# An encoder layer on one core: the square sum of r's first half goes from TensorE to GpSimd, and VectorE's work around the second up stage is reordered

## The chip, the cores and the metric

One core of one Trainium2 chip. The metric is the device time of one execution in microseconds. The kernel before has a median of 1065.91 us over three runs (1065.86 to 1066.0).

## The reference

One layer of a streaming encoder on 544 tokens (512 of a prompt and 32 of a sample), width 1024, all in float32:

```
r = x + 0.5 * rms_norm(swiglu_ffn(rms_norm(x, g1), w_up1, w_down1), g1_post)
z = rms_norm(r, g_mix) @ w_in                 # windowed attention and a gated short convolution
r = r + rms_norm(concat(norm_A(attn), norm_B(conv)) @ w_out, g_mix_post)          # stage "out"
r = r + 0.5 * rms_norm(swiglu_ffn(rms_norm(r, g2), w_up2, w_down2), g2_post)      # stages "up2", "down2"
r = r + rms_norm(sigmoid(rms_norm(r, g_ple) @ w_gate) * (p @ w_proj), g_ple_post)
```

`swiglu_ffn(x)` is `(silu(x @ gate) * (x @ up)) @ down` with a hidden width of 2816. Between the stages "out" and "up2" three things are needed of each token: the norm of out's result y, the sum r = r + norm(y), and the norm of the new r. The change lies there.

## The kernel before

**Tiling.** Features lie on the 128 partitions and tokens in the free dimension: r is eight tiles k = 0 to 7 of 128 features, each with two halves of 272 tokens, A and B. A float32 product is made of three matmuls in a reduced float32 type: each operand is split into a high part and the rest (w_hi x_hi, w_hi x_lo, w_lo x_hi). ScalarE makes the high parts (`split_hi` for weights, `high` for x), VectorE the rests (`split_lo`, `chain_lo`, whose results are x_lo). The normalising factor of x is not in x: the products are scaled by it afterwards on VectorE (`up_scale` makes tG and tU from the four PSUM banks, and by that frees the bank), so a matmul of up2 needs r alone, and its scaling needs the norm.

**Square sums.** ScalarE squares a tile of 272 tokens into one of two buffers `sq` (`square`, L684). GpSimd adds it to `ssq` (`add`, L602; the first of a sum is a copy, L599) and counts in the semaphore `summed`. ScalarE's square number s waits for `summed >= s - 1`, since the buffer must be free. When a sum is complete, TensorE multiplies `ssq` by a matrix of ones (`all_sums`, L1753), which adds over the partitions; ScalarE takes the root (`root`, L692), VectorE the reciprocal (`invert`, L1159). Sum 10 is y of half A, 11 is y of half B, 12 is r of half A, 13 is r of half B. **Sum 12 is the exception**: GpSimd is passed by. TensorE itself adds the eight squares in PSUM, one matmul by ones for each (`add_square`, L1760), with hooks in its passes over x_hi.

**Order around the change.** Every engine has a queue written out by hand.
- TensorE: the four products of out's half B (their ends are 3 us apart), then up2. For half A: a pass over x_hi of units 0 and 1, with sum 11 ahead of its fifth tile, a pass of units 2 and 3, both with the `add_square` hooks (all L1774), then the pass over x_lo for each of the four units (L1782). For half B (units 4 to 7): x_hi of all, then sum 13, then x_lo. After that products of 24 matmuls in turn (L1731, L1732, L1733), pair by pair: pairs 4 to 9, each of two products. A pair's product waits for the scaling (`g_scaled`, `u_scaled`) of the pair two before it. Behind pair 9 stand the seven products a round of a Strassen-like scheme (`seven`) for the rest of the hidden width, whose token operands (`scaled_x` and `token_block` on VectorE, L1212 and L1226) must be ready by then.
- ScalarE: evacuates out's products (square and copy of y), with r's high parts A between; then `root` 11, eight squares of r's half A, `root` 12, then high part and square of each tile of half B (`chain`), silu of pairs 0 and 1, and so on.
- VectorE: `chain_r` of half A (scale y by the norm, L1167, then r = y * gain + r, L1174), two `split_lo`, then reciprocal 11, `chain_r` of half B; after its tile 3 come the eight x_lo of half A, reciprocal 12 and `up_scale` of pair 0, after its tile 4 `up_scale` of pair 1. Then `scaled_x` of the block B21 (four instructions), the eight x_lo of half B, reciprocal 13, `split_lo`, `up_scale` of pairs 2 and 3, three more `split_lo` and token work, and `up_scale` of pair 4.

`up_stage` serves both up stages; `ci` is 0 in the first and 2 in the second.

Of the kernel before, what the change touches and what calls it, by code (L numbers as in the profile page):

```python
# [17 lines left out]
def encoder_layer(nc, t):  # L18
# [121 lines left out]


    SUM_HALF = [A, B] + [A, B, A, B] + [A, A, B, B] + [A, B, A, B] + [A, A, B, B] + [A, B]
    SUMMED = [8, 16, 30, 40, 38, 48, 52, 62, 60, 64, 76, 80, 88, 96, 110, 118, 120, 128, 140, 144]

    PLE_UNITS = [(i, h) for g in (0, 2) for h in (A, B) for i in (g, g + 1)]

# [6 lines left out]
    with ctx:  # L153
# [196 lines left out]

        TASKS_A = NCH + (HT - 1) // CHUNK + 1

        OUT_SQUARES = [(kind, h, k) for kind, n in (("y", KD // 2), ("r", KD)) for h in (A, B) for k in range(n)]

        MIX_SQUARES = [(0, k) for k in range(KA)] + [(n, k) for n in (1, 3) for k in (0, 1)] + \
                      [(2, k) for k in range(KA)] + [(n, k) for n in (1, 3) for k in (2, 3)]
# [100 lines left out]
        def sum_place(n):  # L457

            return 2 * (n % 2) if SUM0["mix"] <= n < SUM0["out"] else SUM_HALF[n]


        OWN_SUM = SUM0["out"] + 2

        def sums_asked(n):

            return n + 1 - (n > OWN_SUM)

        def sum_bank(n):

# [112 lines left out]
        def _(pool):  # L582
# [65 lines left out]
            for h in (A, B):  # L648
                run(SQ0["out"] + 4 * h, h, 4, True)
            for j, (kind, h, k) in enumerate(OUT_SQUARES):  # L650
                if (kind, h) == ("r", A):
                    continue
                add(SQ0["out"] + 8 + j, ssq[:, h, :], kind == "r" and k == 0)
            weight_sums(1, "up2")
            last_group(groups(SQ0["down2"], 2, DOWN_GROUPS), 2)
# [6 lines left out]
        def _(act):  # L662
# [22 lines left out]

            def root(n, size):

                if n == OWN_SUM:
                    act.wait_ge(summed, SUMMED[n])
                else:  # L690
                    act.wait_ge(sum_done, sums_asked(n))
                nc.scalar.activation(sum_bank(n), sum_bank(n), ACT.Sqrt, bias=eps[:], scale=1.0 / size)\  # L692
                    .then_inc(rooted, 1)

# [366 lines left out]
            def highs(first, last):  # L1061
                for k in range(first, last):
                    act.wait_ge(r_ready, 16 + k + 1)
                    high(2, k, A)

            out_evacuate(1, A, 0), out_evacuate(1, A, 1)
            split_hi(c1)
            out_evacuate(1, A, 2)
# [3 lines left out]
            split_hi(c1 + 2)  # L1072
            out_evacuate(1, B, 0)
            highs(0, 1)
            out_evacuate(1, B, 1)
            highs(1, 4)
            out_evacuate(1, B, 2)
            split_hi(c1 + 3)
            highs(4, KD)
            out_evacuate(1, B, 3)  # L1080
            root(SUM0["out"] + 1, D)
            for k in range(KD):
                square(half(r, k, A), squares + OUT_SQUARES.index(("r", A, k))).then_inc(squared, 1)
            root(SUM0["out"] + 2, D)

            act.wait_ge(state_stored, 16 * 6)
# [25 lines left out]

            def token_roots(k):

                act.wait_ge(sum_done, sums_asked(SUM0["ple"] + k))
                tiles, columns = TOKEN_SUMS[k]
                whole = [tt for tt in tiles if tt < XT - 1]
                i = nc.scalar.activation(rms_tok[:, whole[0]:whole[-1] + 1], columns[:, 0:len(whole)], ACT.Sqrt,
                                         bias=eps[:], scale=1.0 / D)
                if XT - 1 in tiles:  # L1120
                    i = nc.scalar.activation(rms_tok[0:DEC, XT - 1:XT], columns[0:DEC, len(whole):len(whole) + 1],
                                             ACT.Sqrt, bias=eps[0:DEC], scale=1.0 / D)
                i.then_inc(tok_rooted, 1)
# [25 lines left out]
        def _(dve):  # L1149
# [193 lines left out]
            def up_stage(n, s, d, ci, y, n_pre):  # L1343

                c0 = C0[s]
                if ci:
                    chain_r(ci, B, y, n_pre - 2, {3: lambda: (chain_lo(ci, A), invert(n_pre - 1, rpre[:, A, :]),
                                                              up_scale(s, 0)), 4: lambda: up_scale(s, 1)})
                    scaled_x(n, ci, B21)
                    chain_lo(ci, B)  # L1350
                    up_hidden(s, 0)
                else:
                    up_scale(s, 0)
                    chain_lo(ci, B, range(0, 2))
                    up_scale(s, 1)
                    up_hidden(s, 0), up_hidden(s, 1)
                    chain_lo(ci, B, range(2, KD))
                    scaled_x(n, ci, B21)
                invert(n_pre, rpre[:, B, :])
                if ci:  # L1360
                    up_hidden(s, 1)
                    split_lo(c0 + 4)
                    up_scale(s, 2)
                else:
                    up_scale(s, 2)
                    split_lo(c0 + 4)
                up_scale(s, 3)
                split_lo(c0 + 5)
                up_hidden(s, 2), up_hidden(s, 3)
                split_lo(c0 + 6), split_lo(c0 + 7)  # L1370
                if not ci:
                    rest_of_gains()
                scaled_x(n, ci, B11, B12)
                token_block(n, 0)
                scaled_x(n, ci, B22)
                up_pair(s, 4)
                token_block(n, 1), token_block(n, 2)
                token_block(n, 3)
                up_pair(s, 5)
                token_lo(n, 0), token_lo(n, 1)  # L1380
                up_pair(s, 6)
                split_lo(c0 + 8), split_lo(c0 + 9)
                first_sums(n, s, 0)
                token_lo(n, 2)
                up_pair(s, 7)
                block_lo(n, s, 0, 0)
                block_lo(n, s, 0, 1)
                block_lo(n, s, 0, 2)
                up_scale(s, 8)
                up_hidden(s, 8)  # L1390
                up_scale(s, 9)
                token_lo(n, 3)
                up_hidden(s, 9)
                token_lo(n, 4)
                block_lo(n, s, 0, 3)
                jobs(n, s, d)
# [256 lines left out]
            split_lo(EARLY[0]), split_lo(EARLY[1])  # L1653
            chain_r(2, A, y_out, SUM0["out"])
            split_lo(EARLY[2]), split_lo(EARLY[2] + 1)

            up_stage(1, "up2", "down2", 2, y_out, SUM0["out"] + 3)
            down_stage("down2", 3)
# [63 lines left out]
        def _(pe):  # L1722
# [15 lines left out]
            def all_sums(n, size=None):  # L1738
# [12 lines left out]
                    pe.wait_ge(attn_ready, NTASK)  # L1751
                src = ssm[:, k, :] if 0 <= k < 4 else ssq[:, SUM_HALF[n], :]
                nc.tensor.matmul(sum_bank(n), ones[:], src, start=True, stop=True).then_inc(sum_done, 1)  # L1753

            def add_square(n, k):

                s = SUMMED[n] - KD + k
                pe.wait_ge(squared, s + 1 - KD)
                pe.wait_ge(summed, s)
                nc.tensor.matmul(sum_bank(n), ones[:], sq[:, s % 2, :], start=(k == 0), stop=(k == KD - 1))\  # L1760
                    .then_inc(summed, 1)

            def hi_pass(pair, high, h, wait, hooks={}, ks=range(KD)):

# [93 lines left out]
            def up_stage(n, s, ci, hooks_hi, second, n_pre, after_b=lambda: None):  # L1858
                for h in (A, B):
                    units = [(U0[s] + 2 * p + m, C0[s] + 2 * PAIRS[p][0] + m, lambda p=p, m=m: up_ready(s, p, m))  # L1860
                             for p in (2 * h, 2 * h + 1) for m in range(2)]
                    if h == A and ci:
                        def high(k, h):
                            return x_high(ci, k, h)

                        def adds(first, last, at):
                            return {at + k - first: lambda k=k: add_square(OWN_SUM, k) for k in range(first, last)}
                        hi_pass(units[0:2], high, A, lambda k: pe.wait_ge(*hi_mark(ci, A, k)),
                                {4: lambda: all_sums(n_pre - 2), **adds(0, 2, 6)})
                        hi_pass(units[2:4], high, A, lambda k: None, adds(2, KD, 0))  # L1870
                        for m, (u, c, _) in enumerate(units):
                            lo_pass(u, c, lambda k, h: x_low(ci, k, h), A,
                                    None if m else lambda k: pe.wait_ge(x_ready, 16 * ci + k + 1))
                    elif h == A:

                        for m in range(4):
                            if m == 2:
                                turn_x(XT - 2), turn_x_sample()
                            hi_pass(units[m:m + 1], lambda k, h: x_high(0, k, h), A,
                                    lambda k: None if m else pe.wait_ge(*hi_mark(0, A, k)))  # L1880
                        first_sums()
                        for m, (u, c, _) in enumerate(units):
                            lo_pass(u, c, lambda k, h: x_low(0, k, h), A,
                                    None if m else lambda k: pe.wait_ge(x_ready, k + 1))
                    else:
                        if ci:
                            first_units(units, ci, B, lead=LEAD, between=lambda: all_sums(n_pre))
                        else:
                            first_units(units, ci, B, {}, {0: after_b}, between=lambda: all_sums(n_pre))
                for p in range(4, 2 * NCL):  # L1890
# [345 lines left out]
```

## Time and profile before

| what | value |
|---|---|
| median of three runs | 1065.91 us |
| the profiled execution | 1065.69 us |
| its span in the trace | 1063.9 us |
| outside the span | 1.8 us |
| TensorE, granted clock over the span | 0.994 |
| TensorE busy | 1035.0 us, 97% |
| VectorE busy | 701.3 us, 66% |
| ScalarE busy | 511.1 us, 48% |
| GpSimd busy | 278.5 us, 26% |

Times in the trace are from the start of the span. In a timeline each row is a start, a duration, the engine, line, operation and tiles, then in square brackets how long the engine had been idle and what ended that. Rows of several instructions ("x4") run from the start of the first to the end of the last. Ends overlap the next start by some 0.08 us on VectorE and ScalarE, and by more on TensorE, whose matmuls are pipelined; so spacing of starts is what an instruction costs its queue. The second up stage begins at 592.8 us.

### The profile page before, as it was taken

The numbers are of one execution on the slowest core, as the hardware profiler recorded it, in microseconds if no ns is written. First come the engines' busy times: TensorE is split into PE (matmuls) and PEld (weight loads), VectorE is DVE, ScalarE is ACT, GpSimd is POOL, SyncE is SP. The second block draws the span as 40 slices with busy tenths as digits, with TensorE's granted clock in tenths as the row PEclk, the third lists the DMA queues.
The fourth block names the chain that finished last, engine by engine and source line by source line (L and its number), as shares of the span: only waits on it lengthen the run. The fifth ranks groups of instructions, "written<-read, shape, count | busy, mean of one in ns | idle before, by whom it ended". The sixth has DMA issues, their size and how long they took to land.

```text
span 1063.9 us, 20130 instructions
## 1 busy us (share of the span) xinstructions
PE 1035.0 (97%) x8109; PEld 1012.7 (95%) x8109; DVE 701.3 (66%) x1053; ACT 511.1 (48%) x931; POOL 278.5 (26%) x214
## 2 busy tenths in 40 slices
PE   6999999999999999999999999999999999999896
PEld 6999999999999998888899999999999999999896
DVE  5889877777511269677695998977777841118743
ACT  5554555556412254434455555555555632126653
POOL 3114343431111142000323201443434021114311
PEclk9999999999999999999999999999999999999998
DMA  8214343335323303221234121443333632233002
GB/s 247 81 41 115 93 111 92 108 94 146 105 63 109 79 23 84 79 67 34 70 97 120 40 80 47 113 120 91 109 93 94 166 108 63 74 99 97 25 1 85
DMA packets 182679, 94.77 MB, mean 89 GB/s; under 512 B 11768, under 2 KB 180928, under 8 KB 182592
## 3 DMA queue, kind: packets, MB, share of 16 engines
q1 hardware_dynamic: 182576, 93.56, 31.8%
q8 instruction: 61, 1.00, 0.4%
q14 instruction: 26, 0.21, 0.1%
q10 hardware_dynamic: 16, 0.00, 0.0%
HBM read 91.15 MB, written 2.50 MB: 88 GB/s over the span
## 4 chain that ended last, share of the span: by engine, by line
PE 84%; DVE 9%; issue 2%; ACT 2%; POOL 1%; DMA 1%; SPq 1%; DVEq 0%; POOLq 0%; ACTq 0%
PE bank L1731 14%; PE bank L1733 14%; PE bank L1732 14%; PE bank L1852 9%; PE bank L1855 9%; PE bank L1854 9%; PE bank L1774 5%; PE bank L1782 2%; PE misc L1933 2%; PE misc L1852 1%; PE misc L1855 1%; PE misc L1854 1%; DVE x_lo L1183 1%; PE misc L2008 1%; DVE w_split L1153 1%
## 5 line engine op out<-in xcount | busy, mean ns | idle before, releaser
L1733 PE MATMUL bank<-h_hi,w_split 128*128 128x272 f32 x704 | 204.0, 290 | 0.0
L1731 PE MATMUL bank<-h_hi,w_split 128*128 128x272 f32 x704 | 203.0, 288 | 0.0
L1732 PE MATMUL bank<-h_lo,w_split 128*128 128x272 f32 x704 | 202.2, 287 | 0.0
L1153 DVE TENSOR_TENSOR w_split<-raw,w_split 128x1408 fp32r<-128x1408 f32 (+2 forms) x66 | 98.7, 1507 | 146.0 <-ACT w_split L679 146.0
L602 POOL TENSOR_TENSOR ssq<-ssq,sq 128x272 f32<-128x272 f32 x105 | 101.9, 970 | 234.9 <-ACT sq L684 228.9
L1732 PEld LDWEIGHTS bank<-h_lo,w_split 128*128 128x128 f32 x704 | 132.6, 188 | 0.1
L1731 PEld LDWEIGHTS bank<-h_hi,w_split 128*128 128x128 f32 x704 | 132.4, 188 | 0.1
L1733 PEld LDWEIGHTS bank<-h_hi,w_split 128*128 128x128 f32 x704 | 132.3, 188 | 0.0
L1852 PE MATMUL bank<-t_hi,even_blocks 128*128 128x272 f32 x432 | 125.3, 290 | 0.2
L1855 PE MATMUL bank<-t_hi,even_blocks 128*128 128x272 f32 x432 | 125.0, 289 | 0.0
L1854 PE MATMUL bank<-t_lo,even_blocks 128*128 128x272 f32 x432 | 124.4, 288 | 0.0
L632 POOL TENSOR_TENSOR s_rest<-s,raw_up 128x512 f32<-128x512 f32 x32 | 70.6, 2206 | 199.6 <-DVE s L1245 199.6
L679 ACT ACTIVATE w_split<-raw 128x1408 fp32r<-128x1408 f32 (+2 forms) x66 | 81.1, 1240 | 83.2 <-PE bank L1733 76.7
L1852 PE MATMUL bank<-t_hi,odd_blocks 128*128 128x272 f32 x384 | 111.5, 290 | 2.0 <-ACT kept L749 1.1
L1855 PE MATMUL bank<-t_hi,odd_blocks 128*128 128x272 f32 x384 | 111.1, 289 | 0.0
L1854 PE MATMUL bank<-t_lo,odd_blocks 128*128 128x272 f32 x384 | 110.5, 288 | 0.0
L1732 PE MATMUL bank<-x_lo,w_split 128*128 128x272 f32 x320 | 92.2, 288 | 0.0
L1852 PEld LDWEIGHTS bank<-t_hi,even_blocks 128*128 128x128 f32 x432 | 81.3, 188 | 0.6 <-issue 0.6
L1854 PEld LDWEIGHTS bank<-t_lo,even_blocks 128*128 128x128 f32 x432 | 81.4, 188 | 0.0
L1855 PEld LDWEIGHTS bank<-t_hi,even_blocks 128*128 128x128 f32 x432 | 81.3, 188 | 0.0
L1852 PEld LDWEIGHTS bank<-t_hi,odd_blocks 128*128 128x128 f32 x384 | 72.2, 188 | 2.7 <-issue 1.5
L1731 PE MATMUL bank<-x_hi_a,w_split 128*128 128x272 f32 x240 | 71.9, 299 | 1.5 <-DVE tG L1667 1.4
(253 smaller groups left out, 2626.3 us busy)
## 6 DMA issues: line engine op xcount, KB each, us to landing
raw_up<-w_ffn_gate_up SPq DMA_DIRECT2D x88, 512.0 KB, 5.1
raw<-w_ffn_down SPq DMA_DIRECT2D x32, 704.0 KB, 4.9
raw<-w_in SPq DMA_DIRECT2D x14, 512.0 KB, 4.2
raw<-w_ple_gate SPq DMA_DIRECT2D x8, 512.0 KB, 3.8
x_tok<-x_prompt SPq DMA_DIRECT2D x4, 512.0 KB, 5.1
raw<-w_in SPq DMA_DIRECT2D x8, 256.0 KB, 3.8
raw<-w_out SPq DMA_DIRECT2D x16, 128.0 KB, 3.5
raw<-w_out SPq DMA_DIRECT2D x8, 256.0 KB, 4.1
```

What stands on the lines that cost most here:

```text
L602: nc.gpsimd.tensor_tensor(dst, dst, sq[:, s % 2, :], ALU.add).then_inc(summed, 1)
L632: nc.gpsimd.tensor_tensor(s24(j)[:, 0, :], s31[:, 1, :], a[:, 0, :], ALU.add).then_inc(s24_made[n], 1)
L679: nc.scalar.activation(chunk_part(c, 0), chunk_raw(c), ACT.Copy).then_inc(hi_made, 1)
L1153: nc.vector.tensor_tensor(chunk_part(c, 1), chunk_raw(c), chunk_part(c, 0).bitcast(F32), ALU.subtract).then_inc(lo_made, 1)
L1731: nc.tensor.matmul(psum(u), wh, hi, start=(k == 0), stop=False)
L1732: nc.tensor.matmul(psum(u), wh, lo, start=False, stop=False)
L1733: mm = nc.tensor.matmul(psum(u), wl, hi, start=False, stop=(k == n - 1))
L1774: nc.tensor.matmul(psum(u), chunk_part(c, part)[:, k, :], high(k, h), start=(k == 0 and part == 0), stop=False)
L1782: mm = nc.tensor.matmul(psum(u), chunk_part(c, 0)[:, k, :], low(k, h), start=False, stop=(k == KD - 1))
L1852: nc.tensor.matmul(out, hi[:, k, :], x_h, start=(k == 0 and p in (1, 2, 7)), stop=False, skip_group_check=True)
L1854: nc.tensor.matmul(out, hi[:, k, :], x_l, start=False, stop=False, skip_group_check=True)
L1855: mm = nc.tensor.matmul(out, lo[:, k, :], x_h, start=False, stop=(k == 3), skip_group_check=True)
```

## The change

- TensorE: the eight `add_square` are gone. In their place one `all_sums` (sum 12) stands ahead of tile 5 of the second pass over x_hi of half A. Sum 13 stands behind the first x_lo pass of half B in place of ahead of it.
- GpSimd adds the eight squares of r's half A, as it does in all other sums. The order in which squares are added is: y of half B tile 0, r A 0, y B 1, r A 1 to 3, y B 2, y B 3, r A 4 to 7, r B 0 to 7. Sum 11 is therefore complete at `summed` 84 (80 before).
- ScalarE: the eight squares of r's half A are spread: tile 0 behind the first high part, tiles 1 to 3 behind high parts 1 to 3 and ahead of the evacuation of out's unit B 2, tiles 4 and 5 ahead of `root` 11, and 6 and 7 behind it.
- VectorE: four of the x_lo of half A come ahead of reciprocal 11, four remain behind tile 3 of `chain_r`. `scaled_x` of B21 moves from ahead of the x_lo of half B to behind `up_scale` 3 and its `split_lo`. The `split_lo` of chunk 4 comes ahead of reciprocal 13, and no longer behind it.

```diff
-    SUMMED = [8, 16, 30, 40, 38, 48, 52, 62, 60, 64, 76, 80, 88, ...]
+    SUMMED = [8, 16, 30, 40, 38, 48, 52, 62, 60, 64, 76, 84, 88, ...]
-        OUT_SQUARES = [(kind, h, k) for kind, n in (("y", KD // 2), ("r", KD)) for h in (A, B) for k in range(n)]
+        OUT_SQUARES = [("y", A, k) for k in range(KD // 2)] + \
+                      [("y", B, 0), ("r", A, 0), ("y", B, 1)] + [("r", A, k) for k in range(1, 4)] + \
+                      [("y", B, 2), ("y", B, 3)] + [(kind, h, k) for kind, h, a in (("r", A, 4), ("r", B, 0))
+                                                    for k in range(a, KD)]
 # GpSimd
             for j, (kind, h, k) in enumerate(OUT_SQUARES):
-                if (kind, h) == ("r", A):
-                    continue
                 add(SQ0["out"] + 8 + j, ssq[:, h, :], kind == "r" and k == 0)
 # ScalarE
             highs(0, 1)
+            squares_of_r(0, 1)
             out_evacuate(1, B, 1)
             highs(1, 4)
+            squares_of_r(1, 4)
             out_evacuate(1, B, 2)
             split_hi(c1 + 3)
             highs(4, KD)
             out_evacuate(1, B, 3)
+            squares_of_r(4, 6)
             root(SUM0["out"] + 1, D)
-            for k in range(KD):
-                square(half(r, k, A), squares + OUT_SQUARES.index(("r", A, k))).then_inc(squared, 1)
+            squares_of_r(6, KD)
             root(SUM0["out"] + 2, D)
 # VectorE
             split_lo(EARLY[2]), split_lo(EARLY[2] + 1)
+            chain_lo(2, A, range(0, 4))
...
                 if ci:
-                    chain_r(ci, B, y, n_pre - 2, {3: lambda: (chain_lo(ci, A), invert(n_pre - 1, rpre[:, A, :]),
-                                                              up_scale(s, 0)), 4: lambda: up_scale(s, 1)})
-                    scaled_x(n, ci, B21)
+                    chain_r(ci, B, y, n_pre - 2, {3: lambda: (chain_lo(ci, A, range(4, KD)),
+                                                              invert(n_pre - 1, rpre[:, A, :]), up_scale(s, 0)),
+                                                  4: lambda: up_scale(s, 1)})
                     chain_lo(ci, B)
                     up_hidden(s, 0)
+                    split_lo(c0 + 4)
...
                 if ci:
                     up_hidden(s, 1)
-                    split_lo(c0 + 4)
                     up_scale(s, 2)
...
                 up_scale(s, 3)
                 split_lo(c0 + 5)
+                if ci:
+                    scaled_x(n, ci, B21)
 # TensorE
-                                {4: lambda: all_sums(n_pre - 2), **adds(0, 2, 6)})
-                        hi_pass(units[2:4], high, A, lambda k: None, adds(2, KD, 0))
+                                {4: lambda: all_sums(n_pre - 2)})
+                        hi_pass(units[2:4], high, A, lambda k: None, {5: lambda: all_sums(n_pre - 1)})
-                            first_units(units, ci, B, lead=LEAD, between=lambda: all_sums(n_pre))
+                            first_units(units, ci, B, {}, {0: lambda: all_sums(n_pre)}, lead=LEAD)
```

## Rows read from the trace of the kernel before

**Rows 1.** The page's busy times: engine, us (share of the span), instructions.
```profile
PE 1035.0 (97%) x8109; PEld 1012.7 (95%) x8109; DVE 701.3 (66%) x1053; ACT 511.1 (48%) x931; POOL 278.5 (26%) x214
```
**Rows 2.** The chain that ended last, 592 to 620: start, us, what.
```profile
592.82 2.02 PE bank L1774 x16
...
596.32 0.63 PE misc L1760 x2
...
603.22 0.46 PE misc L1760 x2
...
609.14 8.00 PE bank L1774 x64
```
**Rows 3.** Timeline of TensorE, the first product of pair 4.
```profile
622.60 0.37 PE L1731 MATMUL bank<-x_hi_up,w_up 128*128 128x272 f32 x1 [0.75 <-DVE tG L1193]
```
**Rows 4.** Timeline of ScalarE, 587 to 596.
```profile
587.42 1.53 ACT L697 ACTIVATE x_hi_up<-r,gT 128x272 fp32r<-128x272 f32 x3
...
589.85 0.40 ACT L684 ACTIVATE sq<-bank 128x272 f32<-128x272 f32 x1 [0.90 <-PE bank L1733]
...
590.42 1.06 ACT L679 ACTIVATE w_up<-raw_up 128x1024 fp32r<-128x1024 f32 x1
591.37 1.75 ACT L697 ACTIVATE x_hi_up<-r,gT 128x272 fp32r<-128x272 f32 x4
593.03 0.38 ACT L684 ACTIVATE sq<-bank 128x272 f32<-128x272 f32 x1
...
595.35 0.46 ACT L692 ACTIVATE misc<-misc,eps 128x272 f32<-128x272 f32 x1 [1.65 <-PE misc L1753]
```
**Rows 5.** Timeline of GpSimd, 587 to 606.
```profile
587.33 0.77 POOL L602 TENSOR_TENSOR ssq<-ssq,sq 128x272 f32<-128x272 f32 x1 [2.23 <-ACT sq L684]
...
593.49 1.03 POOL L602 TENSOR_TENSOR ssq<-ssq,sq 128x272 f32<-128x272 f32 x1 [2.17 <-ACT sq L684]
605.00 0.41 POOL L599 COPY ssq<-sq 128x272 f32<-128x272 f32 x1 [10.48 <-ACT sq L684]
```
**Rows 6.** Timeline of VectorE, 595 to 634.
```profile
595.85 1.87 DVE L1159 RECIPROCAL misc<-misc 128x272 f32<-128x272 f32 x1 [1.96 <-ACT misc L692]
597.75 0.79 DVE L1167 TENSOR_TENSOR y_out<-misc,y_out 128x272 f32<-128x272 f32 x2
...
601.14 3.38 DVE L1183 SCALAR_TENSOR_TENSOR x_lo_up<-r,gT,x_hi_up 128x272 fp32r<-128x272 f32 x8
...
611.78 3.29 DVE L1212 SCALAR_TENSOR_TENSOR t_raw<-r,gT,rpre 128x272 f32<-128x272 f32 x4
...
622.02 0.43 DVE L1193 TENSOR_TENSOR tG<-bank,rpre 128x272 f32<-128x272 f32 x1
...
632.15 1.73 DVE L1212 SCALAR_TENSOR_TENSOR t_raw<-r,gT,rpre 128x272 f32<-128x272 f32 x4
633.80 0.43 DVE L1193 TENSOR_TENSOR tG<-bank,rpre 128x272 f32<-128x272 f32 x1
```
**Rows 7.** Timelines of VectorE and GpSimd at the first up stage, 16 to 24.
```profile
17.65 3.79 DVE L1183 SCALAR_TENSOR_TENSOR x_lo_up<-r,gT,x_hi_up 128x272 fp32r<-128x272 f32 x4
...
16.87 6.92 POOL L602 TENSOR_TENSOR ssq<-ssq,sq 128x272 f32<-128x272 f32 x6 [1.21 <-ACT sq L684]
```
**Rows 8.** Timeline of VectorE ahead of the mix stage, at 395.
```profile
394.97 2.77 DVE L1183 SCALAR_TENSOR_TENSOR x_lo<-r,gT,x_hi_a 128x272 fp32r<-128x272 f32 x4
```
**Rows 9.** Windows: stretch, us, busy us of PE, PEld, DVE, ACT, POOL; PE clock; DMA.
```profile
622.60:634.68 12.08, 12.08 (x96) 12.08 (x97) 11.94 (x23) 4.18 (x7) 0.00 (x0) 1.00 0.61 175
...
994.00:996.00 2.00, 0.00 (x0) 0.03 (x1) 2.00 (x6) 1.71 (x5) 1.64 (x2) 1.00 0.00 0
...
997.00:998.00 1.00, 1.00 (x7) 1.00 (x6) 1.00 (x2) 0.67 (x2) 0.86 (x2) 0.50 0.00 0
```
**Rows 10.** Timeline of TensorE at two of its longer gaps.
```profile
996.00 4.81 PE L1774 MATMUL bank<-x_hi_a,w_split 128*128 128x272 f32 x24 [2.98 <-DVE tG L1667]
...
1042.83 1.06 PE L1933 MATMUL misc<-ident,y_gain 128*128 128x128 f32 x8 [1.74 <-issue]
```

More of the change, by code:

```diff
@@ L142, in encoder_layer @@
     SUM_HALF = [A, B] + [A, B, A, B] + [A, A, B, B] + [A, B, A, B] + [A, A, B, B] + [A, B]
-    SUMMED = [8, 16, 30, 40, 38, 48, 52, 62, 60, 64, 76, 80, 88, 96, 110, 118, 120, 128, 140, 144]
+    SUMMED = [8, 16, 30, 40, 38, 48, 52, 62, 60, 64, 76, 84, 88, 96, 110, 118, 120, 128, 140, 144]
     PLE_UNITS = [(i, h) for g in (0, 2) for h in (A, B) for i in (g, g + 1)]
@@ L459, in sum_place @@
             return 2 * (n % 2) if SUM0["mix"] <= n < SUM0["out"] else SUM_HALF[n]
-        OWN_SUM = SUM0["out"] + 2
-        def sums_asked(n):
-            return n + 1 - (n > OWN_SUM)
         def sum_bank(n):
@@ L686, in root @@
             def root(n, size):
[L688 to L691, printed above, removed]
+                act.wait_ge(sum_done, n + 1)
                 nc.scalar.activation(sum_bank(n), sum_bank(n), ACT.Sqrt, bias=eps[:], scale=1.0 / size)\
@@ L1064, in highs, with squares_of_r @@
                     high(2, k, A)
+            def squares_of_r(first, last):
+                for k in range(first, last):
+                    square(half(r, k, A), squares + OUT_SQUARES.index(("r", A, k))).then_inc(squared, 1)
             out_evacuate(1, A, 0), out_evacuate(1, A, 1)
@@ L1113, in token_roots @@
             def token_roots(k):
-                act.wait_ge(sum_done, sums_asked(SUM0["ple"] + k))
+                act.wait_ge(sum_done, SUM0["ple"] + k + 1)
                 tiles, columns = TOKEN_SUMS[k]
@@ L1753, in all_sums @@
                 nc.tensor.matmul(sum_bank(n), ones[:], src, start=True, stop=True).then_inc(sum_done, 1)
[L1755 to L1761, printed above, removed]
             def hi_pass(pair, high, h, wait, hooks={}, ks=range(KD)):
@@ L1864, in high @@
                             return x_high(ci, k, h)
-                        def adds(first, last, at):
-                            return {at + k - first: lambda k=k: add_square(OWN_SUM, k) for k in range(first, last)}
                         hi_pass(units[0:2], high, A, lambda k: pe.wait_ge(*hi_mark(ci, A, k)),
-                                {4: lambda: all_sums(n_pre - 2), **adds(0, 2, 6)})
-                        hi_pass(units[2:4], high, A, lambda k: None, adds(2, KD, 0))
+                                {4: lambda: all_sums(n_pre - 2)})
+                        hi_pass(units[2:4], high, A, lambda k: None, {5: lambda: all_sums(n_pre - 1)})
                         for m, (u, c, _) in enumerate(units):
```

## The prediction

> **What bounds the kernel now.** First the page: TensorE is busy 97% of the span [rows 1], so a change is worth what it takes from TensorE's queue, less what TensorE newly waits. Second the chain that ended last, between 592.8 and 620 us: only TensorE stands in it, the matmuls of up2 and between them those of L1760, which the change removes [rows 2]. Third TensorE's timeline: the first idle time of the stage comes at 622.60, 0.75 us, ended by VectorE's tG [rows 3]; then there is none up to pair 6, twelve microseconds with 96 matmuls and VectorE busy 11.94 of 12.08 [rows 9]. So TensorE bounds this stretch with VectorE close behind it, and the question is whether VectorE and ScalarE can feed a TensorE that has less to do.
>
> Two prices come first. A matmul of 272 tokens costs the queue 0.125 us (64 in 8.00, 16 in 2.02); one with ones in full float32, two records, costs 0.46 [rows 2]. From 592.82 to 622.60 TensorE has 192 matmuls (24.0 us), sums 11 and 13 (0.92) and the eight `add_square` (0.63 and seven of 0.46, 3.85), 28.8 of 29.8 us. Some 1.0 us is waiting, behind the x_lo pass.
>
> **What the change takes and adds on TensorE.** Out go 3.85 us, in comes one sum, 0.46: -3.39. The rest of the sum is waits. I follow the queues from 592.82 with the durations of the rows; a chain that crosses engines costs 0.04 to 0.15 us a step, as the gaps between such rows show (a root at 595.35 to 595.81, reciprocal at 595.85 [rows 4, 6]).
>
> **Wait 1, TensorE for sum 11 (an added wait, nothing hides it).** Before, ScalarE squared y's tile B 2 at 589.85 and B 3 at 593.03; between lie a weight split and four high parts, all back to back [rows 4]. Now r's squares 1 to 3 stand ahead of B 2. High part 3 ends at 588.95 [rows 4]; the third square must wait until GpSimd has added the first of them, and B 2's until the second is added, at 0.77 an add and 0.08 between [rows 5]: about 591.1, so 1.25 later than 589.85. B 3's square moves to 594.3, its add starts at 594.7 and takes 1.03 as the same add did before [rows 5], and TensorE can start sum 11 near 595.9. It wants it at 592.82 + 2.02 = 594.84. Wait: 1.05 us. Bounds: 0.5, if the adds run at 0.77, and 1.7.
>
> **Wait 2, TensorE for x_lo of half A (the large one).** What counts is when VectorE starts reciprocal 11. Before it waited 1.96 us for the root and started at 595.85 [rows 6]; that idle time is what the four x_lo are to fill. With the root ready at 595.9 + 0.46 + 0.5 it could start at 596.9. But GpSimd, which was idle for 10.48 us here [rows 5] because TensorE did the sum, now adds nine tiles in 589.3 to 599.6, five of them in a row from 594.7. Where GpSimd adds, VectorE's instructions with two SBUF tensors are slow: eight x_lo took 3.38 with GpSimd idle [rows 6], four took 3.79 beside a row of adds, 0.95 each against 0.41 [rows 7], and the four `scaled_x` at 611.78 took 3.29 against 1.73 later [rows 6]. By 0.54 for an instruction that meets an add (0.95 less 0.41), I estimate 0.9 for three adds beside `chain_r` A and 0.4 for one beside the weight splits, so VectorE is at its x_lo at 595.2 (593.89 before); four at 0.95 end at 599.0. That is 3.15 later than before. The reciprocal ends at 600.9, r's tile B 3 at 604.8 (3.4 as before, and 0.5 for one add beside it), x_lo A 4 at 605.75; the sum 12 is complete, so ScalarE and GpSimd work on half B's squares here, and x_lo 5 is slowed too. x_lo A 7 ends at 607.7. TensorE is through with both x_hi passes at 592.82 + 8.0 + 0.92 + 1.05 = 602.8 and wants x_lo 4 at 603.3; it gets the last at 607.85, against 603.7 unhindered. Wait: 4.15 us, nearly all in two pieces of 2.6 and 1.0. Bounds: 0.3 if VectorE isn't slowed (reciprocal 11 at 596.9), 5.2 if its splits are slowed by a second add.
>
> The Trainium skill speaks of this too: "GPSIMD Engine Reference", section Specifications, has GpSimd's SBUF interfaces shared with VectorE, in contention with VectorE's instructions of two SBUF inputs. By that rule moving eight adds from PSUM to GpSimd is itself the cost, and the reciprocal and the scalings out of PSUM stay unhurt, as these rows have it; without the rule the sum would be that of the second rival below.
>
> **Wait 3, TensorE for tG of pair 2.** Sum 13 now stands behind one x_lo pass; three are left, 3.0 us. From its end: root 0.5, reciprocal 1.88, `up_hidden` 0.36, tG 0.35, hand-overs 0.2, together 3.3. Wait 0.3 against 1.0 before: -0.7. VectorE has done everything ahead of reciprocal 13 by then (by the same spacings its x_lo of half B end near 619.2, the weight split near 620.7, and the root comes at 620.9), so TensorE leads here, but by little. Bounds 0 and 1.3.
>
> **Wait 4, TensorE for tG of pair 4 (from moving B21).** Before, VectorE started tG of pair 2 at 622.02 and of pair 4 at 633.80, 11.78 later, all busy [rows 6]. The four `scaled_x` now stand in that stretch: 1.65 at their spacing there (GpSimd is idle; 3.29 if it were not). TensorE started 0.58 behind the start of a tG [rows 3, 6]. So pair 6 can start 13.43 + 0.58 = 14.01 behind tG of pair 2, and TensorE is there at 0.58 + 12.08 (two pairs [rows 9]) = 12.66. Wait: 1.35, whenever the stretch starts. Pairs 7 to 9 have more room than this costs, and the products behind pair 9 start from TensorE's last product as before.
>
> Sum 13's move, the semaphore values and the loads cost nothing: the loads of the next chunks land long before their splits, and SP's queue has no DMA moved. (Were that cover gone, TensorE would wait on a weight split and not on tG.)
>
> **Sum:** -3.39 + 1.05 + 4.15 - 0.7 + 1.35 = +2.45 us at the start of pair 6, carried to the end, since the stretch behind it is TensorE's. Against the profiled execution, 1065.69, that is 1068.15; against the median, 0.2 higher, 1068.4.
>
> **Rivals.**
> - *The clock falls in wait 2.* A gap of 2.98 us was followed by a granted clock of 0.50, the 1.2 GHz level, and 24 matmuls in 4.81 us, about 1.7 more than at 2.4 GHz; a gap of 1.74 was followed by none [rows 9, 10]. Wait 2 has 2.6, one matmul, and 1.0, between the two. If it falls, +1.7: 1070.1. For it: 4.2 us of nearly nothing. Against: matmuls between. By the Trainium skill's "TensorE: Matmul & The Clock Gate", Part 1, the idle state is the throttled one and activity releases it, which would give this case.
> - *VectorE isn't slowed, so not slower than before.* The place is the four x_lo ahead of reciprocal 11, the price 0.54 each and the same again behind. If adds and x_lo fell side by side unhindered, reciprocal 11 starts at 596.9, wait 2 is 0.3, and the sum is -3.39 + 1.05 + 0.3 - 0.7 + 1.35 = -1.4: 1064.5. It decides at about 597.7, that is, if the four x_lo take no more than 2.5 us. For it: adds are often 1.0 apart and leave gaps. Against: rows 7. With wait 1 gone too, -2.5: 1063.4.
> - *Half of it.* Four x_lo took 2.77 us ahead of the mix stage, beside the last adds of a row [rows 8]. Then reciprocal 11 starts 1.0 earlier, wait 2 shrinks by that and by a part of the second group's: +0.9, 1066.8.
> - *That the sum isn't moved* can't be: the matmuls of L1760 are gone from the program.
>
> **How the numbers follow.** About 0.2% (2.1 us) is what a measurement of this kernel tells from no change. The forecast, +2.45 with 1.7 to 3.4: 0.34, of it 0.22 over 2.1. The clock: 0.26. Half: 0.20. Not slowed: 0.20, of it 0.06 faster by over 2.1. So faster 0.06, same 0.46, slower 0.48. The range goes from the second rival's 1064.3 to 1070.6 behind the first one's; cases of both signs hold chances, and the forecast's own range is 1067.6 to 1069.3.
>
> **What would show it.** Right: no L1760; TensorE idle about 1 us ahead of sum 11; x_lo of half A near 0.95 each beside GpSimd's adds; reciprocal 11 some 3 us later than 595.85; TensorE waiting 3 to 4 us for x_lo_up in its first x_lo pass; 1.3 us idle ahead of pair 6's first product. The clock: a window of 0.5 near 608 to 612. Wrong: x_lo at 0.41 to 0.6 each, reciprocal 11 at 597, and pair 6 starting ahead of 634.7. What would upset all of it is a wait behind pair 9, where token blocks or GpSimd's weight sums come late.

## The result

| | median, us | runs |
|---|---|---|
| before | 1065.86 (1065.63 to 1066.45) | 7 |
| changed | 1069.69 (1068.49 to 1070.29) | 7 |

The changed kernel takes 1.0035 of the time before, 95% interval 1.0026 to 1.0045: 3.8 us slower. The profiled execution took 1069.69 us, its span is 1067.9 (1063.9 before). It is slower by more than the forecast of 2.45, above the forecast's own range (1067.6 to 1069.3) and close to the first rival, which had the same course and the fall of TensorE's clock on top (1070.1).

The page's busy times, engine, us (share), instructions, answer to [rows 1]:

```profile
PE 1034.4 (97%) x8095; PEld 1011.8 (95%) x8095; DVE 705.5 (66%) x1053; ACT 510.9 (48%) x931; POOL 284.3 (27%) x222
```

GpSimd has eight instructions and 5.8 us more, which is the sum it took over. VectorE has the same 1053 instructions and 4.2 us more: the same work, done more slowly. TensorE's busy time hardly fell, though eight sums became one: 3.4 us of work went and some 1.7 us of matmuls at half the clock came. Where the rest is, the page doesn't show.

**Where VectorE's time went.** Its timeline answers to [rows 6]:

```profile
592.42 1.80 DVE L1151 TENSOR_TENSOR w_early<-raw_up,w_early 128x1024 fp32r<-128x1024 f32 x1
594.14 1.21 DVE L1151 TENSOR_TENSOR w_up<-raw_up,w_up 128x1024 fp32r<-128x1024 f32 x1
595.27 3.77 DVE L1181 SCALAR_TENSOR_TENSOR x_lo_up<-r,gT,x_hi_up 128x272 fp32r<-128x272 f32 x4
598.97 1.85 DVE L1157 RECIPROCAL misc<-misc 128x272 f32<-128x272 f32 x1
...
604.79 2.73 DVE L1181 SCALAR_TENSOR_TENSOR x_lo_up<-r,gT,x_hi_up 128x272 fp32r<-128x272 f32 x4
607.45 1.84 DVE L1157 RECIPROCAL rpre<-misc 128x272 f32<-128x272 f32 x1
...
614.83 4.95 DVE L1181 SCALAR_TENSOR_TENSOR x_lo_up<-r,gT,x_hi_up 128x272 fp32r<-128x272 f32 x8
...
622.49 1.86 DVE L1157 RECIPROCAL rpre<-misc 128x272 f32<-128x272 f32 x1 [1.22 <-ACT misc L684]
...
627.27 1.73 DVE L1210 SCALAR_TENSOR_TENSOR t_raw<-r,gT,rpre 128x272 f32<-128x272 f32 x4
```

and GpSimd's to [rows 5]:

```profile
589.57 3.56 POOL L599 TENSOR_TENSOR ssq<-ssq,sq 128x272 f32<-128x272 f32 x4 [1.25 <-ACT sq L679]
594.99 4.68 POOL L599 TENSOR_TENSOR ssq<-ssq,sq 128x272 f32<-128x272 f32 x5 [1.86 <-ACT sq L679]
603.06 0.41 POOL L596 COPY ssq<-sq 128x272 f32<-128x272 f32 x1 [3.39 <-ACT sq L679]
603.81 1.68 POOL L599 TENSOR_TENSOR ssq<-ssq,sq 128x272 f32<-128x272 f32 x2 [0.34 <-ACT sq L679]
```

The reader is to lay the second over the first. Five adds run from 594.99 to 599.67, and in just that stretch four x_lo take 3.77 us where four of the eight took 1.7 before. The reciprocal, out of PSUM, keeps its 1.85. It starts at 598.97 in place of 595.85. The second four, from 604.79, meet the adds of half B and take 2.73.

The move of B21 shows the same thing. Its four `scaled_x` stood beside adds of half B's squares before and took 3.29 [rows 6]; at 627.27 they take 1.73. The eight x_lo of half B now stand beside those adds (three from 614.70), and went from 3.38 to 4.95. Of the instructions with two SBUF tensors, the adds slow whichever lie beside them.

**What TensorE waited for.** Its timeline, rows with an idle time; the lines are the sum by ones (L1754), the x_lo pass (L1775) and the first products of pairs 4 and 6 (L1732). Three rows without idle time are with them: the start of the stage, of the x_lo pass of half A and of the x_hi passes of half B (L1767):

```profile
592.74 2.19 PE L1767 MATMUL bank<-x_hi_up,w_early 128*128 128x272 f32 x16
596.07 0.70 PE L1754 MATMUL misc<-ssq,ones 128*128 128x272 f32 x2 [1.14 <-issue]
...
603.10 0.66 PE L1775 MATMUL bank<-x_lo_up,w_early 128*128 128x272 f32 x4
605.84 0.80 PE L1775 MATMUL bank<-x_lo_up,w_early 128*128 128x272 f32 x2 [2.08 <-DVE x_lo_up L1181]
607.17 4.13 PE L1775 MATMUL bank<-x_lo_up,w_early 128*128 128x272 f32 x18 [0.53 <-DVE x_lo_up L1181]
...
612.34 1.91 PE L1767 MATMUL bank<-x_hi_up,w_early 128*128 128x272 f32 x14
...
625.32 0.36 PE L1732 MATMUL bank<-x_hi_up,w_up 128*128 128x272 f32 x1 [0.35 <-DVE tG L1191]
...
638.66 0.40 PE L1732 MATMUL bank<-x_hi_up,w_up 128*128 128x272 f32 x1 [1.06 <-DVE tG L1191]
```

The profile names no releaser for the first wait ("issue"); the queue has a wait for `summed` there, and the add that completes it is the first of the five from 594.99. The windows that answer to [rows 9] (stretch, us, busy us of PE, PEld, DVE, ACT, POOL, granted clock, DMA):

```profile
607.00:608.00 1.00, 0.81 (x4) 0.60 (x5) 1.00 (x3) 0.00 (x0) 0.00 (x0) 1.00 0.00 0
608.00:609.00 1.00, 1.00 (x7) 1.00 (x7) 1.00 (x1) 0.00 (x0) 0.00 (x0) 0.60 0.00 0
609.00:610.00 1.00, 1.00 (x7) 1.00 (x6) 0.97 (x3) 0.00 (x0) 0.00 (x0) 0.50 0.00 0
...
611.00:612.00 1.00, 1.00 (x8) 1.00 (x7) 0.44 (x1) 0.76 (x2) 0.17 (x1) 0.69 0.00 0
```

Behind the wait for x_lo the granted clock is 0.50, the 1.2 GHz level, from 608.2 to 611.6: in 609 to 610 seven matmuls stand where ten or eleven stand at full clock. Pair 6 starts at 638.66. In the kernel before its first matmul, the 97th from 622.60 on, is this row:

```profile
634.78 0.29 PE L1731 MATMUL bank<-x_hi_up,w_up 128*128 128x272 f32 x1
```

(The prediction had 622.60 + 12.08 = 634.68 from the window in [rows 9].) That is 3.9 later, and the span is 4.0 longer. All of it is made between 592.7 and 638.7, and nothing behind gives any of it back.

### The profile page after: what moved, and what is told of

Same layout as the page of the kernel before. It is cut to its first block, busy times and chain, and to the rows that moved or that the text cites. A ratio compares the mean times of both kernels' runs of the same rounds, so it can differ in the third digit from the quotient of the medians.

```text
span 1067.9 us, 20111 instructions
## 1 busy us (share of the span) xinstructions
PE 1034.4 (97%) x8095; PEld 1011.8 (95%) x8095; DVE 705.5 (66%) x1053; ACT 510.9 (48%) x931; POOL 284.3 (27%) x222
## 4 chain that ended last, share of the span: by engine, by line
PE 80%; DVE 13%; issue 2%; ACT 2%; POOL 1%; DMA 1%; SPq 1%; DVEq 0%; POOLq 0%; ACTq 0%
PE bank L1732 14%; PE bank L1734 13%; PE bank L1733 13%; PE bank L1845 9%; PE bank L1847 9%; PE bank L1848 9%; PE bank L1767 4%; PE misc L1923 2%; PE bank L1775 2%; DVE r L1172 1%; PE misc L1847 1%; PE misc L1845 1%; PE misc L1848 1%; DVE x_lo L1181 1%; PE misc L1998 1%
## 5 line engine op out<-in xcount | busy, mean ns | idle before, releaser
L1732 PE MATMUL bank<-h_hi,w_split 128*128 128x272 f32 x704 | 203.1, 288 | 0.0
L599 POOL TENSOR_TENSOR ssq<-ssq,sq 128x272 f32<-128x272 f32 x112 | 106.9, 954 | 237.7 <-ACT sq L679 230.5
L1732 PEld LDWEIGHTS bank<-h_hi,w_split 128*128 128x128 f32 x704 | 132.5, 188 | 0.1
L1732 PE MATMUL bank<-x_hi_a,w_split 128*128 128x272 f32 x240 | 71.9, 300 | 1.5 <-DVE tG L1668 1.4
```

Of the source, the lines that this page charges most:

```text
L599: nc.gpsimd.tensor_tensor(dst, dst, sq[:, s % 2, :], ALU.add).then_inc(summed, 1)
L1732: nc.tensor.matmul(psum(u), wh, hi, start=(k == 0), stop=False)
```

## Experiments

Each ratio is against the kernel before, on the same chip. "Changed" stands for the changed kernel.

### GpSimd without the adds

```diff
             for j, (kind, h, k) in enumerate(OUT_SQUARES):
+                if (kind, h) == ("r", A) and k:
+                    s = SQ0["out"] + 8 + j
+                    pool.wait_ge(squared, s + 1 - KD)
+                    pool.wait_ge(summed, s)
+                    nc.gpsimd.memset(idle_word[:], 0.0).then_inc(summed, 1)
+                    continue
```

> The changed kernel, but GpSimd writes one zero to a word of its own in place of adding the squares of r's half A, tiles 1 to 7; all queues, waits and counts stay. (Left out: seven of the eight squares in the norm of r's half A.) Theory (GpSimd's adds slow VectorE's instructions with two SBUF tensors, and the gap that follows lets TensorE's clock fall): the four x_lo ahead of reciprocal 11 take 1.7 us and not 3.77, reciprocal 11 starts near 596.4 and not 598.97, TensorE's waits for x_lo shrink from some 3.5 to 1 or less, no window of 0.5 near 609, pair 6 starts near 634; time 1065.0 to 1065.6, some 4.5 under the changed kernel. Rival (the new order of the squares on ScalarE and the new waits are the cause, not the adds): x_lo near 0.95 each again or reciprocal 11 late all the same, time within 1 us of 1069.7.

Measured: 1064.89 us, ratio 0.9989 (0.9980 to 0.9998), 4.8 under the changed kernel. VectorE:

```profile
593.92 2.24 DVE L1188 SCALAR_TENSOR_TENSOR x_lo_up<-r,gT,x_hi_up 128x272 fp32r<-128x272 f32 x4
596.08 1.85 DVE L1164 RECIPROCAL misc<-misc 128x272 f32<-128x272 f32 x1
```

Reciprocal 11 is back at 596.08, no window between 602 and 614 has a clock under 1.00, and pair 6 starts at 633.36. The four x_lo took 2.24 and not 1.7: the add of y's last square, which is in both kernels, stands at 593.58 for 1.04 us and lies beside the first ones. ScalarE's order, every queue and every count are those of the changed kernel, so it is the adds that slow x_lo.

The edit takes away two things, though: the adds' operand traffic and the time they take. GpSimd's zero takes 0.10 us where an add takes 0.77 or more, so ScalarE gets its buffers sooner, and TensorE hardly waits for sum 11 (it starts at 594.72, 596.07 in the changed kernel). By the table below that is 1.2 us of the 5.2 that pair 6 gains; the other 3.9 are the x_lo and the clock behind them. With this order of the queues it is also the bound of what the change can bring: with the adds for nothing, 1 us.

### Four x_lo back behind tile 3

```diff
-            chain_lo(2, A, range(0, 4))
...
-                    chain_r(ci, B, y, n_pre - 2, {3: lambda: (chain_lo(ci, A, range(4, KD)),
+                    chain_r(ci, B, y, n_pre - 2, {3: lambda: (chain_lo(ci, A),
```

> The changed kernel with the four x_lo back behind tile 3 of r's half B. Theory (the adds run in any case and only meet other instructions): reciprocal 11 starts at 596.9, 2 us earlier, but the eight x_lo now meet the adds of half B's squares, the last ends only some 0.4 us earlier, TensorE waits for x_lo as before in one gap of 1 to 3 us; time 1068 to 1069.5, depending on the clock. Rival (having four x_lo ahead of the reciprocal is the fault, since it puts them beside the adds): what reciprocal 11 gains, 2.1 us and the clock's 1.7, comes back whole, 1066.

Measured: 1069.51 us, ratio 1.0037 (1.0023 to 1.0051), as the changed kernel. VectorE:

```profile
596.69 1.87 DVE L1157 RECIPROCAL misc<-misc 128x272 f32<-128x272 f32 x1 [1.95 <-ACT misc L684]
601.98 5.05 DVE L1181 SCALAR_TENSOR_TENSOR x_lo_up<-r,gT,x_hi_up 128x272 fp32r<-128x272 f32 x8
606.96 1.85 DVE L1157 RECIPROCAL rpre<-misc 128x272 f32<-128x272 f32 x1
```

In this profile the stage starts at 592.14, 0.60 earlier than in the changed kernel's, which has to be taken off every difference. Reciprocal 11 gains 1.7 us, with VectorE idle for 1.95 ahead of it, and the eight x_lo then take 5.05 where they took 3.38 before [rows 6], since the adds of half B's squares are now under way. Reciprocal 12 (607.45 in the changed kernel) gains nothing. The four x_lo ahead are not the fault: in both places they meet adds. The clock fell here too, to 0.50 at 608.2.

### Matmuls that nobody reads, in the gap

```diff
+    FILL = (17, 3, 5, 1)
...
+                        def filler(n):
+                            for _ in range(n):
+                                nc.tensor.matmul(misc[:, 3, HT:HT + 240], chunk_part(C0[s], 0)[:, 0, :],
+                                                 x_high(ci, 0, A)[:, 0:240], start=True, stop=True)
+
+                        def low_ready(k):
+                            if k >= 4:
+                                filler(FILL[k - 4])
+                            pe.wait_ge(x_ready, 16 * ci + k + 1)
                         for m, (u, c, _) in enumerate(units):
-                            lo_pass(u, c, lambda k, h: x_low(ci, k, h), A,
-                                    None if m else lambda k: pe.wait_ge(x_ready, 16 * ci + k + 1))
+                            lo_pass(u, c, lambda k, h: x_low(ci, k, h), A, None if m else low_ready)
```

> The changed kernel, with 26 matmuls whose result nobody reads put on TensorE where it waits for x_lo 4 to 7 of half A (17, 3, 5 and 1 ahead of the tiles, 240 tokens each, about 2.9 us together). They do no work that is wanted. Theory (the clock's fall near 608.3 costs some 1.5 us, since TensorE leads from there to reciprocal 13): no window of 0.5, the time 1.0 to 1.8 under the changed kernel, 1068.0 to 1068.7, though TensorE executes more. Rival (VectorE leads there, and the slow clock costs nothing): equal to the changed kernel within 0.4.

Measured: 1068.4 us, ratio 1.0023 (1.0014 to 1.0033), 1.3 under the changed kernel with 26 matmuls more. The two ratios' intervals overlap (1.0014 to 1.0033 and 1.0026 to 1.0045), so the traces are needed beside them. Its windows, and TensorE's rows:

```profile
608.00:609.00 1.00, 1.00 (x9) 0.93 (x8) 1.00 (x2) 0.00 (x0) 0.00 (x0) 1.00 0.00 0
609.00:610.00 1.00, 1.00 (x10) 1.00 (x9) 0.97 (x2) 0.00 (x0) 0.00 (x0) 1.00 0.00 0
```

```profile
593.17 2.18 PE L1768 MATMUL bank<-x_hi_up,w_early 128*128 128x272 f32 x16
...
611.26 1.93 PE L1768 MATMUL bank<-x_hi_up,w_early 128*128 128x272 f32 x14
...
624.25 0.36 PE L1733 MATMUL bank<-x_hi_up,w_up 128*128 128x272 f32 x1 [0.36 <-DVE tG L1192]
...
637.59 0.39 PE L1733 MATMUL bank<-x_hi_up,w_up 128*128 128x272 f32 x1 [1.04 <-DVE tG L1192]
```

The clock stays at 1.00. The table has the starts of TensorE's rows in four profiles, in us from the start of the stage, which is at 592.66, 592.74, 593.17 and 592.62 in their timelines:

| TensorE starts | before | changed | unread matmuls | without the adds |
|---|---|---|---|---|
| x_lo pass of half A | 12.37 | 10.36 | 10.35 | 9.13 |
| x_hi passes of half B | 16.32 | 19.60 | 18.09 | 14.43 |
| pair 4 | 29.94 | 32.58 | 31.08 | 27.41 |
| pair 6 | 42.12 | 45.92 | 44.42 | 40.74 |

The whole difference of 1.5 us between the second and the third column is made in the x_lo pass of half A, where the clock fell. So 1.3 of the 3.8 us (1.5 in the traces) come with the clock's fall, and 2.5 stay without it.

### TensorE's sum kept, with VectorE's new order

```diff
             for j, (kind, h, k) in enumerate(OUT_SQUARES):
+                if (kind, h) == ("r", A):
+                    continue
...
-            squares_of_r(4, 6)
             root(SUM0["out"] + 1, D)
-            squares_of_r(6, KD)
+            squares_of_r(0, KD)
             root(SUM0["out"] + 2, D)
...
-                                {4: lambda: all_sums(n_pre - 2)})
-                        hi_pass(units[2:4], high, A, lambda k: None, {5: lambda: all_sums(n_pre - 1)})
+                                {4: lambda: all_sums(n_pre - 2), **adds(0, 2, 6)})
+                        hi_pass(units[2:4], high, A, lambda k: None, adds(2, KD, 0))
```

> The changed kernel with sum 12 again by eight matmuls of TensorE, and ScalarE's squares in the order before; VectorE's new order (four x_lo ahead, B21 and a split moved) and sum 13's new place stay. Theory: VectorE's order by itself is worth little, since pair 4's tG paces TensorE: reciprocal 11 starts at 596.4, reciprocal 13 near 619, pair 6 starts 0.7 us later than before; 1066.2 to 1066.9. Rival (VectorE's new order is what costs): 1068 or more.

ScalarE's squares and the order of the adds are those of before here too; VectorE's order and sum 13's place are the changed kernel's. Measured: 1066.38 us, ratio 1.0007 (0.9998 to 1.0016). Reciprocal 11 starts at 596.45, 13 at 619.61, and pair 6 waits 1.00 for tG. VectorE's new order costs 0.4 by the medians and 0.7 by the ratio, whose interval includes no change; so some 3 of the 3.8 us came with the sum.

### B21 back, with the clock's fall and without it

```diff
                 if ci:
...
+                    scaled_x(n, ci, B21)
                     chain_lo(ci, B)
...
                 split_lo(c0 + 5)
-                if ci:
-                    scaled_x(n, ci, B21)
```

> The changed kernel with the four scaled_x of B21 back ahead of the x_lo of half B. Theory (between reciprocal 11 and pair 4's tG VectorE's queue is full, so it matters little where in it they stand): reciprocal 13 starts 1.3 us later, the wait ahead of pair 6 (1.3) is gone and a wait ahead of pair 4 of the same size comes, time within 0.5 of the changed kernel. Rival (the wait ahead of pair 6 is a term of its own, and goes with the move): 1.3 less, 1068.4.

Measured: 1068.52 us, ratio 1.0026 (1.0016 to 1.0036), 1.2 under the changed kernel. The expectation fell, 0.5 was its limit, and the number is the rival's (1068.4). VectorE's row and a window of TensorE's:

```profile
622.33 1.86 DVE L1157 RECIPROCAL rpre<-misc 128x272 f32<-128x272 f32 x1
```

```profile
607.00:608.00 1.00, 1.00 (x4) 0.87 (x5) 1.00 (x2) 0.00 (x0) 0.00 (x0) 0.50 0.00 0
```

Reciprocal 13 starts without idle time, where in the changed kernel VectorE idled 1.22 us ahead of it; so the four `scaled_x` filled a hole. With the unread matmuls, at full clock, that hole is 0.51; the rest of it is the slow clock's, which made TensorE late with the units of half A and with sum 13. That reading was tested by the same move in the kernel with the unread matmuls:

> The kernel with the unread matmuls (e4_fill) and B21 back ahead of the x_lo of half B. Theory: B21's place mattered in e3_b21_back (1.2 us) only because the slow clock made TensorE late and left VectorE idle there, which four scaled_x could fill; at full clock the place is neutral, so the time equals that of e4_fill within 0.4, about 1.0023 of before. Rival (moving B21 costs 1.3 in any case, as the prediction's sum had it): 1.2 under e4_fill, 1.0012 of before.

Measured: 1068.13 us, ratio 1.0021 (1.0012 to 1.0031), against 1.0023 with B21 where the change put it; the expectation held. At full clock the place of B21 is worth nothing that is measured; in the traces pair 6 starts 44.4 us behind the start of the stage in one and 44.3 in the other. The two gains don't add up: the unread matmuls alone give 1.3, B21 back alone 1.2, and both together 1.6.

### A recast by the same theory

From the changed kernel: squares of r's half A behind all of y's, two ahead of `root` 11 and six behind; three x_lo between the two weight splits; B22 behind tG of pair 4; sum 12 behind the passes over x_hi, sum 13 ahead of the x_lo of half B.

```diff
-            split_lo(EARLY[2]), split_lo(EARLY[2] + 1)
-            chain_lo(2, A, range(0, 4))
+            split_lo(EARLY[2])
+            chain_lo(2, A, range(0, 3))
+            split_lo(EARLY[2] + 1)
...
-                scaled_x(n, ci, B22)
                 up_pair(s, 4)
+                if ci:
+                    scaled_x(n, ci, B22)
...
-                        hi_pass(units[2:4], high, A, lambda k: None, {5: lambda: all_sums(n_pre - 1)})
+                        hi_pass(units[2:4], high, A, lambda k: None)
+                        all_sums(n_pre - 1)
```

> The changed kernel recast by the theory: sum 12 stays on GpSimd, but its squares come behind all of y's (two ahead of root 11, six behind it), three x_lo stand between the two weight splits ahead of the row of adds, B22 goes behind tG of pair 4, sum 12 stands behind the passes over x_hi and sum 13 ahead of the x_lo of half B. Theory: no wait for sum 11, reciprocal 11 at 595.9, TensorE waits some 0.8 for sum 12 and 1.2 for x_lo 4 to 7, pair 4 starts near 620.2 (622.6 before), pair 7 1.7 us earlier than before; 1064.0 to 1064.6, under both kernels. Rival (a sum on GpSimd costs VectorE more than it saves TensorE wherever it stands): 1066 or more.

Measured: 1064.62 us, ratio 0.9989 (0.9980 to 0.9998). VectorE, then TensorE's sum 12, pair 4 and pair 7:

```profile
593.01 1.87 DVE L1176 SCALAR_TENSOR_TENSOR x_lo_up<-r,gT,x_hi_up 128x272 fp32r<-128x272 f32 x3
596.16 1.86 DVE L1152 RECIPROCAL misc<-misc 128x272 f32<-128x272 f32 x1
```

```profile
602.71 0.72 PE L1753 MATMUL misc<-ssq,ones 128*128 128x272 f32 x2 [1.05 <-POOL ssq L596]
620.69 0.36 PE L1731 MATMUL bank<-x_hi_up,w_up 128*128 128x272 f32 x1 [0.20 <-DVE tG L1186]
639.44 0.39 PE L1731 MATMUL bank<-x_hi_up,w_up 128*128 128x272 f32 x1 [0.40 <-DVE tG L1186]
```

The row of adds (595.30 to 602.66) now falls on the end of the second split, on reciprocal 11, on the scalings out of PSUM, which keep their 1.86 and 0.43, and on r's tiles of half B, of which three take 0.66 where they took 0.49. Pair 4 starts 1.9 us earlier than before (622.60), 2.2 by the distance from the start of the stage, pair 6 without a wait, and the longest wait of the stretch is 1.05. It is faster than both kernels, than the one before by 0.1%, 1.2 us; the interval leaves no change out by little, and the second run gives the same. The recast moves several parts at once. Three kernels that differ from it by one part or none were run beside one another:

> The recast kernel again, beside the two that differ from it by one part each: 0.9989 of before, as in its first run.

Measured: 1064.4, ratio 0.9988 (0.9979 to 0.9997).

> The recast kernel (e7_recast) with B22 back ahead of tG of pair 4. Theory: VectorE then gates pair 6 by 1.5 us more, of which half comes back at pair 7, so 0.7 to 0.8 over e7_recast. Rival (B22's place is worth nothing, as in e6_b22_late): equal to e7_recast within 0.2.

Measured: 1064.85, ratio 0.9992 (0.9983 to 1.0001): 0.45 over the recast, less than expected, and the intervals overlap. TensorE waits ahead of pair 6 here and not at all in the recast:

```profile
633.85 0.40 PE L1728 MATMUL bank<-x_hi_up,w_up 128*128 128x272 f32 x1 [1.00 <-DVE tG L1186]
```

> The recast kernel with sum 12 by TensorE's eight matmuls: three x_lo between the splits, B21 and B22 late, no adds of r's half A on GpSimd, 3.4 us more on TensorE's queue and hardly a wait. Theory: by the same replay of the queues pair 7 starts 1.0 earlier than before and 0.8 later than in e7_recast, so 1064.9 to 1065.3 against 1065.8 of before. Rival (the sum's place is worth nothing once VectorE's order is right): equal to e7_recast within 0.3.

Measured: 1065.16, ratio 0.9996 (0.9987 to 1.0005): 0.76 over the recast, as expected, though these intervals overlap too. With everything else in order the move of the sum to GpSimd is worth some 0.8 us, of the 3.4 that it takes from TensorE's queue. What the three x_lo between the splits, B21's place and the places of the two sums each add was not tried apart.

### B22 late in the kernel before

```diff
-                scaled_x(n, ci, B22)
+                if not ci:
+                    scaled_x(n, ci, B22)
                 up_pair(s, 4)
+                if ci:
+                    scaled_x(n, ci, B22)
```

> The kernel before with the four scaled_x of B22 behind tG of pair 4 in place of ahead of it, so VectorE is 1.65 us earlier at the point where it gates TensorE. Theory: in the kernel before TensorE itself is just late enough (pair 6 starts without a wait), so nothing changes, 1065.9 within 0.3. Rival (VectorE paces that stretch in the kernel before): up to 1.3 less.

Measured: 1065.69, ratio 1.0 (0.9991 to 1.0009). As expected: in the kernel before, TensorE isn't gated by tG of pair 4.

## Why the prediction was right, and where it was off

The direction and the course were right, and the measured 1069.69 lies within the whole range, 1064.3 to 1070.6. It lies above the forecast's own range: of two cases with the same course the prediction took the one without the clock's fall. The measured terms below are differences of starts in the table above.

- *The two prices* (0.125 us a matmul, 0.46 a sum) and -3.39 on TensorE: TensorE's matmul records fall by 14, seven sums of two records.
- *Wait 1.* Foretold 1.05 at 595.9; sum 11 starts at 596.07. The recorded idle time is 1.14, and 1.3 by the starts (16 matmuls at 0.125 end at 594.74): 0.3 more than foretold. ScalarE's square of y's tile B 3 stands at 594.53 (594.3 foretold), held up by GpSimd's pace.
- *Wait 2.* The four x_lo: 3.8 foretold, 3.77 measured; reciprocal 11: 599.0 and 598.97; last x_lo of half A: 607.7, and reciprocal 12 starts at 607.45. TensorE's wait is 4.15 foretold and 3.6 by the starts: it takes x_lo 4 to 7 at 605.84, 606.25, 607.17 and 607.59. The last comes 0.3 earlier than foretold (607.85), and because of wait 1 TensorE wants it 0.3 later. (Only 2.08 and 0.53 are recorded as idle, since a matmul's record, 0.29 us, reaches beyond its 0.125 in the queue.) The run without the adds shows the cause.
- *Wait 3.* A gain of 0.7 foretold, 0.6 measured (from 3.28 to 2.64 behind the kernel before).
- *Wait 4.* 1.35 foretold, 1.2 by the starts, 1.06 recorded as idle; 1.00 is recorded with TensorE's sum too. 0.1 of the difference is the prediction's start of pair 6 in the kernel before. But as a term of the sum it was wrong in kind: waits 3 and 4 are one budget, VectorE's queue between reciprocal 11 and tG of pair 4. The pair of B21 runs shows it: moved back at full clock, B21 changes nothing.
- *The sum*, +2.45 (its terms give 2.46), is what the kernel with the unread matmuls measures: a ratio of 1.0023 is 2.5 us. That is closer than the terms were: wait 1 was 0.3 too small and wait 2 was 0.6 too large, and the two partly cancel. With the measured terms the sum is 2.1 without the clock, and 3.8 with it.
- *The step that failed* is the choice between the forecast and the first rival in wait 2: the sum has no term for the clock. The matmuls between the pieces of the gap were taken as a reason against its fall. The clock fell in the profiles of the changed kernel, of the one with B21 back, which has the same gap, and of the one with x_lo back, where single matmuls stand up to 0.9 us apart from 602.5 to 607.1; and it cost 1.3 us at the end. The stretches in [rows 9, 10] had a gap of 2.98 with a fall and of 1.74 without (all windows of 1 us from 1040 to 1048 have 1.00); here TensorE had three matmuls in 4.0 us (603.60 to 607.59), which turned out like the first. The rival's price of 1.7 is what the trace shows: 3.4 us at half the clock lose 1.7, and of the 5.3 us that the x_lo pass of half A takes longer than before, 3.6 are waits and 1.7 are left. The unread matmuls give back less than that because with them the pass is 0.2 longer than these figures give without the clock's fall.
- *The rival "not slower"* needed the x_lo unhindered. Without the adds, where wait 1 is gone too, the time is 1064.9; the rival had 1064.5 with wait 1 and 1063.4 without it. The first four x_lo (3.77) decided against it.
- *The rival "half of it"* needed about 2.77 us for the first four x_lo. Only the second four took that, 2.73.

## What to carry to other kernels

Work taken from the busiest engine must be followed to the engine that feeds it next: here GpSimd was free, but its adds fell beside VectorE's instructions, and VectorE was busy 11.9 of 12.1 us in the stretch behind. Lay such adds beside VectorE's instructions that read PSUM (reciprocals, scalings), and not beside those with two SBUF tensors, above all not where TensorE waits for these; that the recast gained by this alone is not shown. And a gap on TensorE that a change opens is to be priced with the clock behind it; here 4.0 us with three matmuls in them cost another 1.3 us. When two profiles are compared, take the start of the stage off first: it lies between 592.14 and 593.17 in these profiles.

## What the runs showed of the hardware

- *GpSimd beside VectorE.* A VectorE instruction of 272 columns with two SBUF tensors takes 0.41 us of its queue alone and 0.93 beside a row of GpSimd's adds (3.70 for four). A weight split of 1024 columns went from 1.21 to 1.80 beside one. In the other direction the adds, 0.77 alone, took 0.94 each (4.68 for five). Reciprocals and scalings out of PSUM kept their times, 1.85 and 0.43, in the recast with adds beside them throughout. That the adds cause it, and not the new order, was shown by taking them away (2.24 for the four). The rows that the prediction read have no reciprocal or scaling beside an add, so that these keep their times is first shown here. Whether it is their reading or their writing wasn't tried.
- *The clock.* It fell to 0.50, though three matmuls were let through within the stretch: at 608.2 in the changed kernel, 0.6 behind the last piece of the gap, and at 606.8 in the kernel with B21 back, ahead of that piece. It was back at 1.00 at 611.6 and 610.2. Matmuls without a use, put in the gap, kept it at 1.00 and gave 1.3 us back. How much of them is needed wasn't tried.
